# Routing of a diffusion layer with mixture of experts on Trainium2: the prompt's tile last, row transposes later, selection in halves

## The reference, cut to what matters

```python
x = x + g1 * mix                       # mix: output projection, 1024 columns
h = rmsnorm(x, norm2_g) * (1 + sc2) + sh2
logits = h @ w_router                  # 16 experts
aff = softmax(logits).transpose()      # (experts, tokens)
gate, idx = top_k(aff, cap)            # cap = 2 * n / 16: 128 sample tokens, 16 prompt tokens an expert
xs = h[idx]
y = (silu(xs @ w1[e]) * (xs @ w3[e])) @ w2[e] * gate
x = x + g2 * scatter_add(idx, y)
```

## Time and profile before

| | |
|---|---|
| median of 3 runs | 1653.16 us (1650.88 to 1654.46) |
| profiled execution | 1656.95 us, its span 1654.9 us |
| PE busy | 1591.8 us (96%) |
| DVE, ACT, POOL busy | 549.8, 416.7, 107.8 us |
| mean granted TensorE clock | 0.982 |

### The profile page before, as it was taken

One profiled execution on the slowest core, in us unless ns is written; L12 is line 12 of the kernel. 1 busy time (PEld: TensorE's weight loads), 2 busy tenths in 40 slices (PEclk: granted clock), 3 DMA queues, 4 the chain that ended last, 5 costly groups with the idle time before them and its releaser, 6 DMA issues.

```text
span 1654.9 us, 26952 instructions
## 1 busy us (share of the span) xinstructions
PE 1591.8 (96%) x10945; PEld 1266.4 (77%) x10945; DVE 549.8 (33%) x1315; ACT 416.7 (25%) x944; POOL 107.8 (7%) x109
## 2 busy tenths in 40 slices
PE   4899998999999999999879999999999999999997
PEld 3644544666666666544469999999999999999996
DVE  3100333474746656214477111111111111111114
ACT  4200101354545545133411111111111111111114
POOL 0003500000000000011100100000000000000000
PEclk9899999999999999999979999999999999999999
DMA  7852002200000000061249777878777878777776
GB/s 311 319 221 91 0 0 77 90 1 6 8 0 13 0 5 1 30 225 51 77 144 363 271 271 287 289 270 303 257 271 276 311 259 301 269 272 268 281 229 242
DMA packets 113514, 288.05 MB, mean 174 GB/s; under 512 B 10095, under 2 KB 15126, under 8 KB 110254
## 3 DMA queue, kind: packets, MB, share of 16 engines
q1 hardware_dynamic: 108702, 269.88, 44.4%
q0 software_dynamic: 4752, 17.30, 3.9%
HBM read 265.53 MB, written 21.64 MB: 174 GB/s over the span
## 4 chain that ended last, share of the span: by engine, by line
PE 93%; DVE 4%; DMA 1%; ACT 1%; issue 0%; SPq 0%; DVEq 0%
PE ps L1058 30%; PE ps L1082 14%; PE ps L711 9%; PE ps L537 9%; PE ps L821 7%; PE ps L768 5%; PE ps L753 4%; PE ps L681 3%; PE ps L598 2%; PE ps L694 1%; PE ps L722 1%; PE ps L550 1%; DVE hreg L1714 1%; PE ps L629 1%; PE ps L1021 1%; PE ps L1013 1%
## 5 line engine op out<-in xcount | busy, mean ns | idle before, releaser
L1058 PE MATMUL ps<-mreg,wreg 128*128 128x144 f32 x4096 | 517.8, 286 | 0.0
L1058 PEld LDWEIGHTS ps<-mreg,wreg 128*128 128x128 f32 x4096 | 509.7, 190 | 0.5 <-issue 0.4
L1082 PE MATMUL ps<-mreg,wreg 128*128 128x144 f32 x2048 | 265.5, 286 | 0.0
L1082 PEld LDWEIGHTS ps<-mreg,wreg 128*128 128x128 f32 x2048 | 258.0, 190 | 0.0
L1919 DVE TENSOR_TENSOR mreg<-ps,mreg 128x144 f32<-128x144 f32 x120 | 36.9, 308 | 442.9 <-PE ps L1058 442.9
L711 PE MATMUL ps<-wreg 128*128 128x512 f32 (+2 forms) x400 | 171.5, 519 | 0.0
L1344 ACT ACTIVATE mreg<-ps 128x144 f32<-128x144 f32 x128 | 37.3, 291 | 445.5 <-PE ps L1058 445.5
L537 PE MATMUL ps<-hreg,wreg 128*128 128x512 f32 (+1 forms) x432 | 143.2, 489 | 0.0
L821 PE MATMUL ps<-wreg,mreg 128*128 128x512 f32 x288 | 132.2, 605 | 2.6 <-DVE wreg L1635 2.6
L753 PEld LDWEIGHTS ps<-const,hreg 128*128 128x128 f32 x648 | 79.8, 140 | 58.5 <-issue 39.0
L537 PEld LDWEIGHTS ps<-hreg,wreg 128*128 128x128 f32 x432 | 70.7, 191 | 70.0 <-issue 69.6
(11 more groups left out here) (254 smaller groups left out, 1183.8 us busy)
## 6 DMA issues: line engine op xcount, KB each, us to landing
wreg<-in_w_e_dram SPq DMA_DIRECT2D x96, 2048.0 KB, 12.2
wreg<-in_w_ada_dram SPq DMA_DIRECT2D x24, 1024.0 KB, 10.0
out_dram<-wreg SPq DMA_DIRECT2D x9, 512.0 KB, 2.6
mreg<-in_x_sample_dram SPq DMA_DIRECT2D x8, 512.0 KB, 7.1
wreg<-in_w_out_dram SPq DMA_DIRECT2D x1, 4096.0 KB, 13.6
wreg<-in_x_sample_dram SPq DMA_DIRECT2D x8, 512.0 KB, 5.4
x_rows<-wreg SPq DMA_DIRECT2D x8, 512.0 KB, 2.9
xn_rows<-wreg SPq DMA_DIRECT2D x8, 512.0 KB, 3.0
```

The costliest lines, as they stand in the source:

```text
L1058: mm = pe.matmul(o[:, 0:CAP], w[s][:, k, (f % 4) * P:(f % 4 + 1) * P], xsT[b][:, k, :], start=(k == 0), stop=(k == KD - 1))
L1082: mm = pe.matmul(bank[4 + dm % 2][:, 0:CAP], w2[f // 4][:, f % 4, dm * P:(dm + 1) * P], hidT[:, f, :], start=(f == 0), stop=(f == 7))
```

## The change

The prompt's tile is last in the order (`ORDER` and `PLACE` go), so each sample tile is one turn earlier, and tiles 4 and 5 have softmax groups of their own. The last two tiles, 7 and 8, have their residual added by DVE in halves (`half_add`, `half_square`, `half_mean` in place of `last_add`, `last_square`, `mean_last`). The row transposes of a turn stand behind `h2_turn` and the first matmul of the odd half, no longer inside the even half. DVE counts for expert 1 as for expert 0, tile group by tile group (`counted(e, g)`): two groups among the projections, three in the first three steps of expert 0. `slots` and `quick_list` work in two halves of the tiles, and expert 0's list is made before the prompt's logits. The prompt's selection, its spreading and its features come at the end, in two halves of 128 slots (half 0 has the slots of experts 0 to 7); the features of half 1 are made in expert 0's step 0, and the gate's transposes in step 2. Expert 1's list is made behind step 3 instead of step 1. The 16 rounds of `sample_picks` go two a step into steps 4 to 7, one into every second block, two behind the blocks and two into expert 1; the three joining steps stand at f = 2, 4, 6 of expert 1 (1, 3, 5 before). DVE's tables for the routing are made, and the first four projection halves evicted, inside the last turn of attention. SP issues the second half of `w2` once the ranks of expert 1 are there, and no longer both halves after its rows.

The diff, cut to its core:

```diff
-ORDER = (0, 1, 2, 3, 8, 4, 5, 6, 7)
-PLACE = {t: p for p, t in enumerate(ORDER)}
 LAST = NT - 1
-R_TILES = (range(0, 4), range(8, 9), range(4, 6), range(6, 7), range(7, 8))
-PROMPT_GROUP = 1
+HALVED = NT - 2
+R_TILES = (range(0, 4), range(4, 5), range(5, 6), range(6, 7), range(7, 8), range(8, 9))
+PROMPT_GROUP = 5
 QUICK = 2
...
             sp.wait_ge(rows_in[0], 16)
-            sp.wait_ge(rows_in[1], 16)
             for s in range(2):
+                if s == 1:
+                    sp.wait_ge(ranked, 2)
                 sp.dma_start(w2[s], w_e2[0, 0, s * 512:(s + 1) * 512, :].rearrange(
                     "(k p) f -> p k f", p=P)).then_inc(w2_in[s], 16)
+            sp.wait_ge(rows_in[1], 16)
             sp.dma_start(final_row, final_norm_g.rearrange("(a d) -> a d", a=1).to_broadcast([P, D])).then_inc(frow_in, 16)
...
             for p in range(3, 8):
                 if p > 3:
-                    out_proj(2 * p, range(0, 4))
-                    if p == 5:
-                        spread_rows(0)
-                    elif p == 6:
-                        prompt_by_expert()
-                    elif p == 7:
-                        prompt_rows()
-                    out_proj(2 * p, range(4, KD))
+                    out_proj(2 * p)
                 h2_turn(p - 1, 0)
                 h2_turn(p - 1, 1)
-                out_proj(2 * p + 1, range(0, 4))
+                out_proj(2 * p + 1, range(0, 1))
+                if p > 4:
+                    spread_rows(p - 5)
+                if p == HALVED:
+                    sample_by_expert(0)
+                out_proj(2 * p + 1, range(1, 4))
                 logits(p - 1)
                 out_proj(2 * p + 1, range(4, 6))
                 by_token(p - 1)
                 out_proj(2 * p + 1, range(6, KD))
-            out_proj(16, range(0, 5))
-            spread_rows(2)
-            out_proj(16, range(5, KD))
+            out_proj(16, range(0, 1))
             h2_turn(7, 0)
+            out_proj(16, range(1, 3))
             h2_turn(7, 1)
+            spread_rows(3)
+            out_proj(16, range(3, 4))
+            logits(7)
+            out_proj(16, range(4, 6))
+            by_token(7)
+            out_proj(16, range(6, KD))
             out_proj(17, range(0, 2))
-            logits(7)
-            out_proj(17, range(2, 3))
-            by_token(7)
-            out_proj(17, range(3, 5))
+            spread_rows(4)
+            out_proj(17, range(2, 5))
             h2_turn(8, 0)
-            out_proj(17, range(5, KD))
-            spread_rows(3)
+            out_proj(17, range(5, 7))
+            sample_by_expert(1)
+            out_proj(17, range(7, KD))
+            quick_list(0)
             h2_turn(8, 1)
             logits(8)
-            prompt_features(range(0, 1))
             by_token(8)
-            prompt_features(range(1, 4))
-            spread_rows(4)
-            prompt_features(range(4, KD))
-            quick_list(0)
-            sample_by_expert()
+            prompt_by_expert()
+            prompt_rows()
...
+                    if first and f == 0:
+                        for k in range(KD):
+                            prompt_features(1, k)
+                    if first and f == 2:
+                        gate_turned()
+                    if first and f == 3:
                         quick_list(1)
-                    if lists and f in (1, 3, 5):
-                        lists[f // 2]()
+                    if lists and f in (2, 4, 6):
...
             act.wait_ge(gain_ok, 2)
-            for p in range(NT - 1):
-                if p in (4, 5, 7):
-                    router_exp((4, 5, 7).index(p))
-                x2_square(p)
-                if p == 4:
-                    rows_evict(0)
-                elif p == 7:
-                    rows_evict(2)
-                x2_root(p)
-                h2_evict(p, 0)
-                h2_evict(p, 1)
-                x2_scale(p)
-            last_square(0)
+            for t in range(HALVED):
+                if t >= 4:
+                    router_exp(t - 4)
+                x2_square(t)
+                if t >= 4:
+                    rows_evict(t - 4)
+                x2_root(t)
+                h2_evict(t, 0)
+                h2_evict(t, 1)
+                x2_scale(t)
+            half_square(7, 0)
             router_exp(3)
+            h2_evict(7, 0)
+            half_square(7, 1)
+            h2_evict(7, 1)
+            rows_evict(3)
+            x2_root(7)
+            act.activation(stat[0:1, 27:28], ones[0:1, 0:1], ACT.Exp)
+            x2_scale(7)
+            router_exp(4)
+            rows_evict(4)
+            act.activation(stat[32:33, 27:28], ones[32:33, 0:1], ACT.Sqrt)
+            half_square(8, 0)
             h2_evict(8, 0)
-            rows_evict(3)
-            last_square(1)
+            half_square(8, 1)
             h2_evict(8, 1)
             x2_root(8)
-            act.activation(stat[0:1, 27:28], ones[0:1, 0:1], ACT.Exp)
-            router_exp(4)
+            act.activation(stat[64:65, 27:28], ones[64:65, 0:1], ACT.Exp)
             x2_scale(8)
-            rows_evict(4)
-
-            for k in range(KD):
-                act.wait_ge(xp_mm, k // 2 + 1)
-                ins = act.activation(xpT[:, k, :], bank[XP_BANK[k // 2]][:, k % 2 * PSLOTS:(k % 2 + 1) * PSLOTS],
-                                     ACT.Identity, bias=modT[:, 1, 24 + k:25 + k], scale=gain2[:, 1, k:k + 1])
-            ins.then_inc(xp_ok, 1)
-            act.wait_ge(turn_mm, 1)
-            act.activation(pick_gate_T, bank[5][:, 0:2 * P].rearrange("p (h t) -> p h t", h=2), ACT.Copy).then_inc(pgt_ok, 1)
-
+            router_exp(5)
...
+            def routing_tables():
+
+                dve.wait_ge(proj_mm, 48)
+                dve.wait_ge(gain_ok, 2)
+                dve.wait_ge(small_in, 16 * 9)
...
+                    elif n == 6:
+                        routing_tables()
...
+                    elif x < 4:
+                        o_evict(x)
...
             for p in range(4, 8):
-                if p == 5:
-                    normalised(0)
-                elif p == 6:
-                    normalised(1)
+                if p > 4:
+                    normalised(p - 5)
                 mean2(p - 1)
                 norm2(p - 1)
-                if p == 6:
-                    prompt_diagonals()
-                elif p == 7:
-                    prompt_picks()
                 o_evict(2 * p)
-                if p == 5:
-                    counted(0)
+                if p == HALVED:
+                    half_add(7, 0)
+                if p > 5:
+                    counted(1, p - 6)
                 logits_out(p - 1)
                 by_token(p - 1)
-                if p in (4, 5, 7):
-                    shifted((4, 5, 7).index(p))
+                shifted(p - 4)
+                if p == HALVED:
+                    probs_out(0)
                 o_evict(2 * p + 1)
-            normalised(2)
-            mean2(7)
+                if p == HALVED:
+                    half_add(7, 1)
+                    normalised(3)
+                    half_mean(7)
+                if p > 4:
+                    counted(0, p - 5)
+            logits_out(7)
             norm2(7)
-            counted(2)
+            counted(0, 3)
+            by_token(7)
+            shifted(4)
+            normalised(4)
             o_evict(16)
-            last_add(0)
-            logits_out(7)
-            by_token(7)
-            shifted(3)
-            normalised(3)
+            half_add(8, 0)
+            counted(0, 4)
+            ranks(0)
+            slots(0)
             o_evict(17)
-            last_add(1)
-            mean_last()
-            counted(3)
+            half_add(8, 1)
+            quick_out(0)
+            probs_out(1)
+            half_mean(8)
             logits_out(8)
             norm2(8)
             by_token(8)
-            shifted(4)
-            normalised(4)
-            counted_last()
-            slots(0)
-            quick_out(0)
-            counted_second(range(0, 4))
-            probs_out(0)
-            probs_out(1)
+            shifted(5)
+            normalised(5)
+            prompt_diagonals()
+            prompt_picks()
...
-            counted_second(range(4, 8))
-            slots(1)
-            at = 0
             for f in range(8):
+                if f < 3:
+                    counted(1, f + 2)
                 hidden(0, f)
-                if f == 1:
+                if f == 2:
+                    ranks(1)
+                    slots(1)
+                elif f == 3:
                     quick_out(1)
-                n = (0, 1, 2, 1, 2, 1, 2, 1)[f]
-                sample_picks(range(at, at + n))
-                at += n
+                elif f > 3:
+                    sample_picks(range(2 * f - 8, 2 * f - 6))
             for dm in range(8):
                 gathered(1, dm, 8 + dm)
-                if at < CAPS // 8:
-                    sample_picks(range(at, at + 1))
```

(48 more changed lines are left out.)

310 lines of the change are left out of this document (151 added, 159 removed).

## The result

| | before | after |
|---|---|---|
| median | 1652.07 us (1650.88 to 1654.46, 4 runs) | 1685.41 us (1678.02 to 1690.49, 4 runs) |
| ratio | | 1.0196, 95% interval 1.0152 to 1.0241 |
| profiled execution, its span | 1656.95, 1654.9 us | 1690.49, 1688.7 us |

What follows compares the result with a forecast made beforehand. PE was taken to be at its limit nearly everywhere, with one clock dip before expert 0. Terms -0.5 + 11.2 - 1.9 - 1.8 = 7.0 sooner, less 3.6 for the clock: 1653.16 - 3.4 = 1649.8 us, range 1644.5 to 1656.

Steps and rivals of the forecast that it cites:

- first part: What bounds the kernel now: PE at its limit nearly everywhere, one clock dip at 820 to 870 us, elsewhere 2.4 GHz matmuls.
- Rival C: Slower: expert 2's gather after the late lists lands 7.5 after issue, PE waits 4.8, clock falls; 1656.4, chance 0.13.
- Start of the routing: Before the per-token matmuls: wait of 2.60 goes, new wait 2.35 behind x2 store, landing unchanged; gain 2.0, tables cost 0.3.
- Tiles 4 to 6: Projection turns ahead of X: later transposes and evictions bring waits, 0.8 in tile 4's turn, 2.3 in tile 5's; sum -2.2.
- X: The end of projection half 14, forecast 0.5 later than before.
- From X to S: From X to the start of expert 0 (S): gather hidden, prompt's chain last; 46.3 against 57.5, gain 11.2.
- Rival D: Prompt's chain ahead of expert 0 is 3 to 4 longer, X to expert 0's start about 50; 1653, chance 0.17.
- Expert 0: Two selection rounds a step make DVE late: waits of 0.35 and 2.35; 54.4 against 52.5, so -1.9.
- Expert 1: Lists turned one step later, so PE waits 1.8 (up to 4.8) for gathered rows.
- The clock: Of four PE waits (2.35, 2.05, 2.35, 1.8) two bring the low clock level: -3.6, net 3.4 sooner.

Runs made afterwards that it cites:

- after_p42: The changed kernel with 42 tiny products (168 instructions) put in an old TensorE wait ahead of the loop; 1655.10 us, ratio 1.0005.

## Why the prediction was wrong
**The failed step** is in its first part: "Elsewhere the chain is matmuls at the 2.4 GHz level". From that the sum went from attention to expert 1 and stopped; everything from expert 2 on was carried over unchanged, a term put at nothing, though the change puts 46 instructions ahead of a loop that touches as many blocks as TensorE can keep. What the runs showed in its place: at its new place the loop is fetched anew at each of five returns, and that costs 39.4 us, against 7.0 for everything that the sum held before the clock. No rival had it either. Rival C, the slower one, had another mechanism, and its wait came at 1.06.

The Trainium skill (Runtime: NRT & Kernel Launch, Instruction fetch mechanics) speaks of this: instructions come in blocks of 16 KiB, 256 each; TensorE's store is 128 KiB, and a taken branch to a block that isn't held waits for a DMA. The runs agree in the block (45 packets for 11,516 instructions) and in the size as far as they go: eight blocks are 128 KiB, and a loop that touches seven is held while one that touches eight is not. The same section says that only the current two pages are held; here seven were.

The risk could have been seen ahead, its size not. The page of before shows 45 packets for a program whose loop is run six times, so the loop was held, and its length says that a move can make it touch one block more. That seven is the limit, and the price, came only with the runs. With both known, a loop somewhere in the good stretch of 128 leaves it by a move of 46 with a chance of 46/128, an estimate of 0.36 at a price of 40 us; even a smaller chance would have asked for a wider range.

**Start of the routing**: the wait of 2.60 went, the new wait for the eviction came at its predicted size, and no low clock behind it; the first per-token matmul came 2.9 sooner (2.0 forecast, and 0.3 lost in attention; 1.1 of it is that attention ended sooner in this execution):
```profile
714.92 0.40 PE L873 MATMUL ps<-quad_sum,creg 128*128 128x16 f32 x2 [2.35 <-DVE creg L1713]
```
Right for the profiled execution, but "I take the same landing" was lucky. The row of before gave one landing, 10.5 us from issue; issued right behind the weights the store took 14.8 after the change, where the wait was 2.35, and 16.7 in after_p42, where it was 4.75. The bounds of 0 to 4.4 had no such case: a new wait behind 4 MB in one queue needs a landing well above the one row as its upper end.

**Tiles 4 to 6**: -1.8 (from 2.9 to 1.1 sooner at X) for -2.2. Tile 5's turn has its wait for the logits' copy behind `counted(1,0)`, 1.95 for 2.05:
```profile
783.16 0.40 PE L873 MATMUL ps<-quad_sum,creg 128*128 128x16 f32 x2 [1.95 <-DVE creg L1713]
...
792.07 1.04 PE L848 MATMUL ps<-const,wreg 128*128 128x128 f32 x8
...
839.17 4.16 PE L1071 MATMUL ps<-mreg,wreg 128*128 128x144 f32 x32 [2.10 <-ACT hreg L1342]
```
**From X to S**: the last two of these rows are 47.1 apart; 46.3 was forecast, 57.5 it was the earlier trace rows. The gather is hidden, the prompt's selection (waits of 2.6 and 2.7) and the features' evictions (2.10) come last, as said. Rival D falls.

**Expert 0**: 56.5 us. The forecast was 54.4, with waits of 0.35 and 2.35; they were 0.50 and 2.06. Of the rest 1.7 is the clock, which was a term of its own, and some 0.5 is left:
```profile
881.53 0.38 PE L1020 MATMUL ps<-const,mreg 128*128 128x128 f32 x1 [2.06 <-DVE mreg L1927]
881.71 3.79 PE L1100 MATMUL ps<-mreg,wreg 128*128 128x144 f32 x16
```
16 pieces in 3.79 instead of 2.13: 1.7. **Expert 1**: 1.3 longer, its wait 1.06 for 1.8. The prediction's own terms (picks at 933.3, gather 0.5 behind, 4.5 to land) add up to 938.3, not 938.8, and so to a wait of 1.3. The 16.4 us of rival D, from 29.3 to 46.3, are 17.0; neither slip moves the sum by over 0.5.

**The clock**: of the four waits of about 2, one lowered it in this execution (two were counted), and in after_p42 two did. Waits of 1.95 and 2.35 left it up, one of 2.06 didn't. The advice of the Trainium skill that the prediction weighed (TensorE: Matmul & The Clock Gate, HAM oscillation) would let all four waits of about 2 pass; the trace again disagrees, here behind 2.06.

At the loop's entry all this stands at 6.2 sooner, against 3.4 forecast and 7.0 with the clock up; 5.1 of it counted from attention's end. Apart from the clock the steps were right within 1 us each. But that too was one execution, with one of the shorter waits for the store. Over 12 timed runs without the stall the changed kernel is at 1655.1 us, ratio 1.0005, and its twin of the old one at 1656.3, ratio 1.0014: 1.2 apart, where the runs of either scatter over 6. So a worth of the change alone isn't shown, nor are the 3.4 that were forecast. The kernel with four of its waits removed stands 11 under the kernel before.

## What to carry to other kernels
Count the instructions of TensorE's loop and the blocks that it touches, and read the row of the instruction queue: many more packets than the program has blocks (90 for 45 here) means that a loop is refetched, and waits with no releaser at its return are the sign in time. Where the loop is near the limit, any edit ahead of it on that engine can change its place, which here cost 40 us or gave them back, and hides what the edit itself does. So compare two versions only with their loops at the same place in a block; small products in an old wait arrange that, at up to 2.5 us here. And put small stores that someone waits for ahead of bulk loads in a queue.

## What the runs showed of the hardware
- TensorE keeps a loop that touches seven blocks of 256 instructions (45 or 46 packets with moves of 0, 24, 36, 184 and 216) and refetches one that touches eight (90 packets with moves of 46, 48 and 144, and with a longer loop): nine packets and 5 us of wait at each return in the changed kernel, 7.9 us with the low clock behind it, 10 at a move of 144, where the loop starts near a block's end. Only TensorE's loop was tried.
- A store of 512 KB took 2.9 us by the median and 14.8 behind 4 MB of weights in one queue, 16.7 in another kernel with the same order; with the first store ahead of the weights the longest of the eight took 6.6. The eight stores of x2 in the changed kernel:
```profile
DMA to landing us min/median/max: 2.6/2.9/14.8
```
